# Expert rows gathered in two rounds, and the second tile's rows added ahead of the last scaling, in a two-layer SSD/attention block with a mixture of experts

## The reference, cut to what matters

```python
def run_block(args):
    xblk, e = args
    return (jax.nn.silu(xblk @ w_gate[e]) * (xblk @ w_up[e])) @ w_down[e]
yb = lax.map(run_block, (xb, block_e)).reshape(cap, d)
return jax.ops.segment_sum(yb * buf_w[:, None], buf_tok, num_segments=t)
...
x_lat = x_lat + g2 * y[: b * n_lat].reshape(b, n_lat, d)     # and the same for x_ctx in layer 0
```

## Time and profile before

| what | value |
| --- | --- |
| median of 3 runs | 1724.54 us (1724.49 to 1726.73) |
| the profiled execution, its own time | 1721.01 us |
| its span, first to last instruction | 1719.2 us |
| mean granted TensorE clock | 0.986 |
| TensorE busy | 1541.8 us (90% of the span) |
| VectorE, ScalarE, GpSimd busy | 621.5, 373.7, 214.5 us |
| moved by DMA | 572.67 MB, mean 333 GB/s |

### The profile page before, as it was taken

One profiled execution on the slowest core, in us unless ns is written; L12 is line 12 of the kernel. 1 busy time (PEld: TensorE's weight loads), 2 busy tenths in 40 slices (PEclk: granted clock), 3 DMA queues, 4 the chain that ended last, 5 costly groups with the idle time before them and its releaser, 6 DMA issues.

```text
span 1719.2 us, 21680 instructions
## 1 busy us (share of the span) xinstructions
PE 1541.8 (90%) x8536; PEld 788.1 (46%) x8536; DVE 621.5 (36%) x1314; ACT 373.7 (22%) x766; POOL 214.5 (12%) x233
## 2 busy tenths in 40 slices
PE   5999999999999899999787788899999998788786
PEld 3434444455444454545344444345565554344343
DVE  2534347888633315312111112748422211111112
ACT  2311147898510100000000000228110000000000
POOL 2000002222110011011001012111001011001001
PEclk9999999999999899999999999999999999999999
DMA  9687668933489699999999999832699999999996
GB/s 373 240 324 276 264 221 209 330 130 127 148 297 281 243 381 425 425 424 425 427 427 427 427 426 418 335 155 71 224 368 423 415 425 426 426 427 425 427 426 255
DMA packets 144656, 572.67 MB, mean 333 GB/s; under 512 B 22939, under 2 KB 79787, under 8 KB 113728
## 3 DMA queue, kind: packets, MB, share of 16 engines
q1 hardware_dynamic: 123888, 524.98, 76.4%
q0 software_dynamic: 14640, 26.03, 4.3%
q10 hardware_dynamic: 6048, 20.58, 3.5%
HBM read 543.01 MB, written 49.25 MB: 344 GB/s over the span
## 4 chain that ended last, share of the span: by engine, by line
PE 56%; DMA 34%; DVE 6%; issue 2%; ACT 1%; SPq 0%; POOL 0%; ACTq 0%; DVEq 0%; POOLq 0%
DMA mem<-in_moe_w_down_dram 18%; PE bank L2066 13%; DMA mem<-in_moe_w_gate_dram 12%; PE bank L640 9%; PE bank L2081 7%; PE bank L1007 6%; PE bank L952 4%; PE bank L2528 3%; PE bank L376 2%; DMA consts<-in_consts_dram 2%; PE bank L2635 2%; PE bank L974 1%; DVE mem L1183 1%; PE bank L2052 1%; PE bank L985 1%
## 5 line engine op out<-in xcount | busy, mean ns | idle before, releaser
L2066 PE MATMUL bank<-mem 128*64 128x256 f32 x4096 | 495.6, 393 | 65.0 <-DMA mem<-in_moe_w_gate_dram 39.0
L2066 PEld LDWEIGHTS bank<-mem 128*64 128x64 f32 x4096 | 284.6, 135 | 273.4 <-DMA mem<-in_moe_w_gate_dram 61.1
L2081 PE MATMUL bank<-mem 128*64 128x512 f32 x1040 | 243.1, 610 | 45.0 <-DMA mem<-in_moe_w_down_dram 41.1
L640 PE MATMUL bank<-mem 128*128 128x512 f32 x384 | 171.2, 598 | 1.2 <-DMA mem<-in_ssd_w_in_dram 1.2
L2263 ACT ACTIVATE mem<-bank 128x256 f32<-128x256 f32 x65 | 25.0, 384 | 668.5 <-PE bank L2066 645.7
L2003 POOL DMA_INDIRECT ys_dram<-mem x61 | 61.2, 1004 | 747.6 <-DVE mem L2345 713.3
L2081 PEld LDWEIGHTS bank<-mem 128*64 128x64 f32 x1040 | 72.2, 139 | 176.1 <-issue 122.2
L2345 DVE TENSOR_TENSOR mem<-bank,mem 128x512 f32<-128x512 f32 x65 | 44.9, 691 | 233.3 <-PE bank L2081 183.3
L2324 DVE TENSOR_TENSOR mem<-mem,bank 128x256 f32<-128x256 f32 x65 | 27.4, 421 | 263.6 <-PE bank L2066 155.7
L640 PEld LDWEIGHTS bank<-mem 128*128 128x128 f32 x384 | 70.8, 190 | 97.9 <-issue 95.8
L952 PE MATMUL bank<-mem 128*128 128x512 f32 x256 | 115.2, 592 | 0.0
(11 more groups left out here) (357 smaller groups left out, 1510.3 us busy)
## 6 DMA issues: line engine op xcount, KB each, us to landing
mem<-in_moe_w_up_dram SPq DMA_DIRECT2D x61, 2048.0 KB, 20.3
mem<-in_moe_w_gate_dram SPq DMA_DIRECT2D x61, 2048.0 KB, 26.4
mem<-in_moe_w_down_dram SPq DMA_DIRECT2D x60, 2048.0 KB, 15.0
mem<-in_mod_w_dram SPq DMA_DIRECT2D x24, 2048.0 KB, 14.4
ys_dram<-consts SPq DMA_DIRECT2D x55, 512.0 KB, 7.5
mem<-in_ssd_w_in_dram SPq DMA_DIRECT2D x10, 2048.0 KB
mem<-ac_dram ACTq DMA_DIRECT2D x32, 512.0 KB, 4.5
mem<-in_ssd_w_out_dram SPq DMA_DIRECT2D x4, 2048.0 KB
```

Of the source, the lines that this page charges most:

```text
L640: mm = nc.tensor.matmul(psum[c % 2][:, :], lhsT=w[:, k, (c % 4) * P:(c % 4 + 1) * P], rhs=aT[0][:, k, :], start=(k == 0), stop=(k == KD - 1))
L2066: mm = nc.tensor.matmul(bank[half * BR:(half + 1) * BR, 0:HF], lhsT=x[:, k], rhs=w[k][:, half::2], start=(k == 0), stop=(k == KD - 1), ski ...
L2081: mm = nc.tensor.matmul(bank[half * BR:(half + 1) * BR, :], lhsT=ht[:, k // 2, k % 2 * BR:(k % 2 + 1) * BR], rhs=w[:, k, half * COLS:(half ...
```

## The change

- GpSimd gathers in two rounds. `NEAR` is 25 in layer 0 and 24 in layer 1. Rows of blocks below `NEAR` are gathered inside the loop, just ahead of the scatter of block `NEAR + 2`, after a wait for the scatters of the blocks below `NEAR`. All other rows are gathered at the old place. Each round issues all 8 (or 4) gathers; a row that belongs to the other round gets an index beyond the bound and is skipped.
- Four small VectorE operations at block 8 of each layer make the two index tables. `cb_in[t]` now counts 64 for each layer in place of 32.
- If overflow blocks run, the near round is gathered again after them, and SyncE waits for the first one before it loads over it.
- VectorE adds tile 1's gathered rows ahead of the last `gated`, in both layers; `norm1_cols_dve` moves there too in layer 0.
- The late adds of tiles 2 and 3 of layer 0 are split into halves and spread over the norm of tiles 0 and 1.
- TensorE starts the first QKV product with the first four columns of `aT[1]`, once both counts are at 5, and waits for 6 only ahead of the other four.

```diff
+        NEAR = [n - 6 for n in LATE]
...
+            def gather_rows(at, done):
+                for t in range(nt):
+                    for k, buf in enumerate(cy):
+                        pool.indirect_dma_start(buf[:, t, :], None, ys_dram[l],
+                                                bass.IndirectOffsetOnAxis(at[:, k, t:t + 1], 0), bounds_check=YS[l] - 1,
+                                                oob_is_err=False).then_inc(done[t], 16)
+
             for j in range(LATE[l]):
+                if j == NEAR[l] + 2:
+                    pool.wait_ge(rt_q, 3 * (t0 + nt) + l + 1)
+                    for i in range(2):
+                        pool.wait_ge(moe_ys[i], 16 * (YB[l][i] + (NEAR[l] + 1 - i) // 2))
+                    gather_rows(r_near, cb_in)
                 scatter(j)
...
             pool.wait_ge(moe_out, l + 1)
-            for t in range(nt):
-                for k, buf in enumerate(cy):
-                    pool.indirect_dma_start(buf[:, t, :], None, ys_dram[l],
-                                            bass.IndirectOffsetOnAxis(r_sloti[:, k, t:t + 1], 0)).then_inc(
-                        cb_in[t], 16)
+            gather_rows(r_far, cb_in)
...
+            def gather_rounds():
+                V, T, cut = nc.vector, slice(0, nt), float(NEAR[l] * BR)
+                link(dve, V.tensor_scalar(r_cut[:, :, T], r_slot[:, :, T], cut, float(SKIP), ALU.is_ge, ALU.mult))
+                V.tensor_tensor(r_near[:, :, T], r_slot[:, :, T], r_cut[:, :, T], ALU.add)
+                link(dve, V.tensor_tensor(r_cut[:, :, T], r_slot[:, :, T], r_cut[:, :, T], ALU.subtract))
+                V.tensor_scalar(r_far[:, :, T], r_cut[:, :, T], float(SKIP), None, ALU.add)
...
                 if j == a + 1:
                     combine_dve(dve, l, 0)
+                    if l == 0:
+                        norm1_cols_dve(dve)
+                    combine_dve(dve, l, 1)
                 gated(j)
-            combine_dve(dve, l, 1)
-            for t in range((3, 2)[l]):
+            for t in range(2):
                 late_add_dve(dve, l, t)
...
-            pe.wait_ge(n1_ea, 6)
-            pe.wait_ge(n1_ed, 6)
             unit_wait(pe, U_QKV)
-            project(0, 0, 0)
+            pe.wait_ge(n1_ea, 5)
+            pe.wait_ge(n1_ed, 5)
+            project(0, 0, 0, range(4))
+            pe.wait_ge(n1_ea, 6)
+            pe.wait_ge(n1_ed, 6)
+            project(0, 0, 0, range(4, KD))
...
-            norm1_cols_dve(dve)
             stream_mean_dve(dve, 0)
+            late_add_dve(dve, 0, 2, [0])
             stream_rows_dve(dve, 0)
-            late_add_dve(dve, 0, 3)
+            late_add_dve(dve, 0, 2, [1])
+            late_add_dve(dve, 0, 3, [0])
             stream_evac_dve(dve, 0)
+            late_add_dve(dve, 0, 3, [1])
```

More of the change, by code:

```diff
@@ L1850, in hybrid_block @@
         LATE = [n - 2 for n in NB]
+        NEAR = [n - 6 for n in LATE]
+        r_near = small(2 * NT, "p (k t) -> p k t", k=2).bitcast(U32)
+        r_far = small(2 * NT, "p (k t) -> p k t", k=2).bitcast(U32)
+        r_cut = small(2 * NT, "p (k t) -> p k t", k=2)
         TOKENS, SPREAD = 8, 28
@@ L1969, in moe_sp @@
             with sp.If(n_ov > 0):
+                for t in range(tiles[l]):
+                    sp.wait_ge(cb_in[t], 64 * l + 32)
                 with sp.Fori(0, n_ov) as i:
@@ L2028, in moe_pool @@
                 pool.wait_ge(ov_st[l], n_ov * 32)
+                pool.sem_inc(ov_list, 1)
+                gather_rows(r_near, [ov_xg[l]] * nt)
+                with pool.Fori(0, n_ov) as i:
+                    pool.wait_ge(ov_xg[l], i * 16 + 16 + 32 * nt)
+                    pool.sem_inc(ov_list, 1)
             pool.wait_ge(moe_xT, 2 * (PB[l] + NPAIR[l]))
@@ L2370, in before @@
                 if j == TOKENS:
+                    gather_rounds()
                     link(dve, nc.vector.tensor_scalar(r_bk[:, :, 0:nt], r_slot[:, :, 0:nt], -float(a * BR), None, ALU.add))
@@ L2426, in combine_dve @@
         def combine_dve(dve, l, t):
-            dve.wait_ge(cb_in[t], 32 * (l + 1))
+            dve.wait_ge(cb_in[t], 64 * (l + 1))
             for k in range(2):
@@ L2434, in combine_dve, with late_add_dve @@
                 ins.then_inc(cb_x, 1)
-        def late_add_dve(dve, l, t):
+        def late_add_dve(dve, l, t, halves=(0, 1)):
             dve.wait_ge(cb_mm, base_t[l] + t + 1)
-            for half in range(2):
+            for half in halves:
                 x = xin[:, t, half * COLS:(half + 1) * COLS]
@@ L2581, in attn_pe @@
             stream_turn_pe(pe, 0)
+            unit_wait(pe, U_QKV)
+            pe.wait_ge(n1_ea, 5)
+            pe.wait_ge(n1_ed, 5)
+            project(0, 0, 0, range(4))
             pe.wait_ge(n1_ea, 6)
             pe.wait_ge(n1_ed, 6)
-            unit_wait(pe, U_QKV)
-            project(0, 0, 0)
+            project(0, 0, 0, range(4, KD))
             project(0, 1, 1)
@@ L2921, in _ @@
             for i in range(NT):
-                sp.wait_ge(cb_in[i], 32)
+                sp.wait_ge(cb_in[i], 64)
             for n in range(U_QKV, U_MOE[1]):
```

## The result

The change costs time: a median of 1738.16 us (1736.91 to 1742.93, 4 runs) against 1725.63 us (1724.49 to 1729.01, 4 runs) of the kernel before on the same chip. The ratio is 1.0080, with a 95% interval of 1.0064 to 1.0096, so slower by 12.5 us by the medians and 13.8 by the ratio. The forecast was 1727.2 us with a range up to 1732.0; the result lies outside it.

A forecast was written before the change was run, and what follows sets the result against it. DMA bandwidth was taken to bound the mixtures, a TensorE and VectorE chain the attention. Layer 0 +1.95 and layer 1 +0.7 make +2.65 us, 1727.2 us against a median of 1724.54; range 1718.5 to 1732.

The forecast's parts named there:

- Costed at nothing: Small VectorE operations, eight more GpSimd issues (10 us in all) and QKV weight loads were taken to add no time.
- sign (2): Between 1000 and 1020 q0 moves about 3 MB, total near 425 GB/s; last scatters of both layers come later.
- Near bytes: Near gathers make every weight behind them later by their bytes: 7.5 us in layer 0, 3.7 in layer 1.
- evenly spread rows: Gathered rows assumed even over blocks: 25 of 33 near in layer 0 (3.18 MB), 24 of 32 in layer 1 (1.57 MB).
- The last downs lose their wait: Last down's weights, 2.96 us late in layer 0 and 2.95 in layer 1, should be there when TensorE is.
- Scaling after the products: VectorE's last scaling starts 5.4 us (layer 0) or 5.15 (layer 1) after D, when the last down may start.
- Behind the scaling, layer 0: From the scaling's start to the mean takes 5.7 us in place of 7.19: -1.5 us.
- From the mean to the projection: Layer 0's projection starts 0.9 us sooner, its first half needing two of VectorE's four evacuations; nothing changes up to the evacuation.
- the order's -2.6: The forecast's terms for VectorE's and TensorE's new order alone, in both layers, add to -2.6 us.
- The slower one: Rival: last weights stay late, so near bytes come on top: +7.35 us, 1731.9; chance 0.22.
- QKV weights: Rival: QKV weights land late and the projection waits, up to +2 us, 1729.2; chance 0.07.
- Near bytes are not free: Answers the faster rival: near bytes cost nothing because queues take up slack, -8.5 us, 1716.0; chance 0.13.

The follow-up runs named there:

- the empty round: The changed kernel with layer 0's cut at slot 0, so its eight near gathers move no row: 1732.17 us, ratio 1.0031 to the kernel before.
- two tiles: The changed kernel with only tiles 0 and 1 in layer 0's near round, tiles 2 and 3 fetched in the far round: 1723.93 us, ratio 0.9993.
- when spread: The changed kernel with the near round cut up, one tile's two gathers ahead of each of several scatters, cut two blocks lower: 1728.31 us, ratio 1.0029.
- 8 KB: The changed kernel with most layer 0 weights loaded in two transfers of 8 KB a partition in place of one of 16 KB: 1734.61 us, ratio 1.0049.
- 4 KB: The changed kernel with most layer 0 weights in four 4 KB loads a partition: 1745.88 us; its control with one gather round and the new order: 1739.86 us.
- the version with the order alone: The changed kernel with one round of gathers at the old place, keeping the new VectorE and TensorE order: 1722.36 us, ratio 0.9985.

## Why the prediction was wrong

**The step that failed** stood under "Costed at nothing": "Eight more issues on GpSimd (0.94 us each and 0.30 between, 10 us in all): the next scatter is a block away, and VectorE waits for it only two blocks later." That counts the issues on the engine and not the packets in its DMA queue. The issues did take 10.3 us, but the queue took nearly 50. Counted from the rows: 8 gathers of 144 packets are 1152; at 24.4 a microsecond beside 16 KB packets they last 47 us. The trace shows it: the input gather ahead of them lands at 1013.8, and they land one after the other until 1061.4, 47.6 us later. The forecast's own sign (2), about 3 MB on q0 between 1000 and 1020, failed by the same step: it is 0.84 MB.

The scatter of block 27 is issued just as that round begins to move (1015.55), and VectorE needs its buffer two blocks later, 31 us (965.12 to 996.25 from the scatter of block 24 to that of block 26 before). It landed 48.6 us after its issue in the change and 41.7 us in the empty round, and VectorE waited; 26.2 us behind two tiles, at most 15.0 when spread and 19.4 in layer 1, and it did not. The count gives the same order: the round lasts 47 us with 16 KB packets and 40 us when empty (1152 at 28.9); 28 us with 8 KB and 19 us with 4 KB (whose traces give no landing), 24 us with two tiles or in layer 1, and 12 us a block when spread.

The price comes in two parts. The empty round has turns without bytes, 10.9 us; the spread round has bytes without the stall, 7.4 us. Together 18.3 us, less the 2.96 that the last down gives back (and that is in the 10.9), is 15.3 us; the change has 15.6 us in that stretch. The input gather is late in the empty round too (TensorE waits another 0.39 us for it), and its share is in these numbers.

**The misreading behind it** is of the earlier trace rows. Equal shares of 44.0% and 42.9% were taken as a rule on bytes. They were measured over a stretch in which q1 has the smaller tail transfers and runs dry, with 614 packets against 1144. The forecast did not ask how long the near round would be in the queue, only how many bytes it takes from the weights.

**Near bytes:** right within a microsecond in both layers: 7.4 us measured in layer 0 in the spread version (7.5 forecast, for some more bytes), 2.7 in layer 1 (3.7 forecast). The guess of evenly spread rows was near: 2.97 MB in layer 0 and 1.63 MB in layer 1, where the forecast took 3.18 and 1.57.

**The last downs lose their wait:** right in layer 0 in every version with a full near round. In layer 1 down starts 5.78 us after up (1723.03 to 1728.81) in place of 8.45, with 0.86 us still waited for DMA. That gives the later blocks back: from block 25's scatter to the end it is 90.98 us against 90.92.

**Scaling after the products:** forecast D + 5.4 and D + 5.15; in the trace D + 5.28 and D + 4.80 (1728.81 to 1733.61). Right within 0.4 us.

**Behind the scaling, layer 0:** forecast 5.7 us from the scaling to the mean, measured 6.98 (1101.79 to 1108.77). The late products took 7.12 us, most of it at the lower clock, which the forecast had not priced. In the version with the order alone, where the low clock falls into down, it is 5.62 (1084.01 to 1089.63), as forecast. From the mean to the projection it is 5.07 us against 5.76 before, 0.7 less where 0.9 was forecast.

**Sum:** the order's -2.6 was right, the bytes' part was right within a microsecond in each layer, and a term of 10.9 us was missing. That the last downs gave back their wait was right too, but in the change the stall alone would have brought it about: in the empty round, where all bytes are far, the last down does not wait for DMA either.

**Rivals.** The slower one said that the last weights stay late; they do not. QKV weights were not late either (issued at 1092.95, the projection waits for VectorE). Near bytes are not free. The mechanism that decided was none of those named.

**Left open:** whether the far gathers' skipped rows cost anything at the end of the layer, where the weights' queue runs dry, was not tried by itself. Nor is it settled why layer 1 pays 2.7 us and not 3.8: it is not for want of near rows (398 of 512, from the 0.47 MB left to the far round). Where the low clock falls is open too: with 8 KB packets TensorE idles the same 2.38 us before the late products, and they take 5.70 us at full clock.

## What to carry to other kernels

Before a transfer is moved into a saturated stretch, count its packets, skipped rows among them, and divide by the turns that the packets beside it leave. That gives the time for which everything behind it in its queue is late. Then look for the next transfer on that queue and for when its buffer is wanted: below that time the move costs its bytes, above it the engines stop. If the move is wanted all the same, spread it so that each piece passes before the buffer comes round again, or move less.

## What the runs showed of the hardware

- A row that an indirect gather skips costs a turn in the queue: 289 packets with 0.00 MB passed in 10 us beside 288 of the weights.
- Packets of two queues pass one to one beside packets four times and twice as large: 243 against 244 with 16 KB, 410 against 408 with 8 KB, both busy all the time. With 4 KB on both sides it was 708 against 611.
- Beside the saturated weights the transfers of GpSimd's queue landed in the order of their issue: eight gathers 5.4 to 6.2 us apart, then the scatter behind them, at 1064.2. Where the weights' queue ran dry they did not: before the change the gather issued at 1064.79 landed after 16.3 us, the one issued at 1066.04 after 13.2.
- The size of packets has a price of its own without any near round: 426 GB/s with 16 KB a partition, 420 with 8 KB, 409 with 4 KB, the last with 16.4 us for the whole kernel.
- A short stretch of low clock can move from one product to the next. Before, and with the order alone, it lay in the last down (5.35 and 5.27 us in place of 3.65); in the change it lay in the products behind it (7.12 us in place of 5.70, clock 0.58), after an idle of 2.38 us. The idle does not decide it: with 8 KB packets the same 2.38 us were followed by 5.70 us at clock 1.00.
